# Halves of the first shift and scale, and one order of products at three attentions' openings, in a three-layer fp32 transformer kernel on one Trainium2 core

## What is computed

```
mod = silu(c) @ ada_w + ada_b;  shift, scale, gate = parts of mod
h = rms_norm(x, gain) * (1 + scale) + shift
x = x + gate * mixer(h)
```

```
logits = q @ k.T + bias (moba, swa), or + F[q] - F[k] (fox)
F = cumsum(log_sigmoid(h @ w_f + b_f))
attn = softmax(masked logits) @ v;  mixer = attn @ w_out
```

## Time and profile before

| what | value |
| --- | --- |
| median of three runs | 1499.24 us (1498.57 to 1499.58) |
| profiled execution, its own time | 1496.46 us |
| its span, first to last instruction | 1494.7 us |
| TensorE busy, mean granted clock | 1408.8 us, 0.982 |
| VectorE, ScalarE, POOL busy | 1085.8, 732.8, 140.3 us |
| moved by DMA | 333.63 MB, mean 223 GB/s |

### The profile page before, as it was taken

The page is one execution under the profiler, slowest core; times in us unless marked ns, Lnnn a source line. Parts: engine busy times, 40 slices in busy tenths (PEclk is TensorE's granted clock), DMA queues, the critical chain, the costliest instruction groups (busy, mean ns, idle before and its releaser), DMA issues.

```text
span 1494.7 us, 18521 instructions
## 1 busy us (share of the span) xinstructions
PE 1408.8 (94%) x7262; PEld 1165.3 (78%) x7262; DVE 1085.8 (73%) x1523; ACT 732.8 (49%) x1036; POOL 140.3 (9%) x199
## 2 busy tenths in 40 slices
PE   2799898999989999988999999999999899999998
PEld 1578888999968888765678887788887676788886
DVE  5857887998988998747478778788877446466444
ACT  3454446444564334667553445643337557554332
POOL 1100100111001221000011110011110100000000
PEclk9899999999999999998999999999999989999999
DMA  9775756877959998440378886688963631475552
GB/s 351 252 221 178 259 180 208 277 266 241 314 161 347 343 355 303 161 167 4 102 242 309 302 294 242 219 302 294 304 235 113 199 113 57 141 253 176 184 183 76
DMA packets 189289, 333.63 MB, mean 223 GB/s; under 512 B 8850, under 2 KB 132478, under 8 KB 188180
## 3 DMA queue, kind: packets, MB, share of 16 engines
q1 hardware_dynamic: 161392, 236.02, 46.9%
q0 software_dynamic: 27232, 96.21, 18.9%
q10 hardware_dynamic: 580, 0.23, 0.1%
HBM read 331.27 MB, written 1.15 MB: 222 GB/s over the span
## 4 chain that ended last, share of the span: by engine, by line
PE 77%; DVE 10%; ACT 5%; DMA 4%; issue 3%; SPq 0%; ACTq 0%; POOL 0%; DVEq 0%; POOLq 0%
PE bank L1473 10%; PE bank L1475 10%; PE bank L1474 10%; PE bank L1436 8%; PE bank L1438 7%; PE bank L1437 7%; DVE lo L968 4%; PE bank L1368 3%; PE bank L1369 3%; PE bank L1370 3%; DMA ada<-in_ada_w 2%; DVE ada_sum L926 2%; PE bank L1601 2%; PE bank L1603 2%; PE bank L1602 2%
## 5 line engine op out<-in xcount | busy, mean ns | idle before, releaser
L968 DVE TENSOR_TENSOR lo<-raw,hi 128x2048 fp32r<-128x2048 f32 x215 | 490.9, 2286 | 83.5 <-ACT hi L535 82.7
L535 ACT ACTIVATE hi<-raw 128x2048 fp32r<-128x2048 f32 x215 | 405.8, 1910 | 31.4 <-DMA raw<-in_w_out 21.1
L1473 PE MATMUL bank<-hi,h_hi 128*128 128x512 f32 x704 | 278.1, 395 | 3.6 <-DVE lo L968 1.9
L1475 PE MATMUL bank<-hi,h_lo 128*128 128x512 f32 x704 | 274.6, 390 | 0.0
L1474 PE MATMUL bank<-lo,h_hi 128*128 128x512 f32 x704 | 274.1, 389 | 0.0
L1436 PE MATMUL bank<-hi,o_hi 128*128 128x512 f32 x504 | 203.7, 404 | 11.6 <-DVE lo L968 9.5
L1438 PE MATMUL bank<-hi,o_lo 128*128 128x512 f32 x504 | 197.3, 391 | 0.0
L1437 PE MATMUL bank<-lo,o_hi 128*128 128x512 f32 x504 | 196.5, 390 | 0.0
L647 ACT ACTIVATE KT<-bank 128x256 f32<-128x256 f32 x88 | 33.8, 384 | 311.9 <-PE bank L1475 311.9
L1473 PEld LDWEIGHTS bank<-hi,h_hi 128*128 128x128 f32 x704 | 132.2, 188 | 33.3 <-DVE lo L968 3.8
L1475 PEld LDWEIGHTS bank<-hi,h_lo 128*128 128x128 f32 x704 | 132.1, 188 | 28.1
(11 more groups left out here) (213 smaller groups left out, 2012.6 us busy)
## 6 DMA issues: line engine op xcount, KB each, us to landing
raw<-in_ffn_w SPq DMA_DIRECT2D x176, 512.0 KB, 5.3
ada<-in_ada_w POOLq DMA_DIRECT2D x100, 512.0 KB, 5.7
raw<-in_ffn_w SPq DMA_DIRECT2D x44, 1024.0 KB, 6.5
V<-in_ada_w POOLq DMA_DIRECT2D x76, 512.0 KB, 5.6
raw<-in_w_up SPq DMA_DIRECT2D x22, 1024.0 KB, 5.8
raw<-in_w_in SPq DMA_DIRECT2D x16, 1024.0 KB, 6.9
raw<-in_fox_w_in SPq DMA_DIRECT2D x12, 1024.0 KB, 5.3
raw<-in_w_down SPq DMA_DIRECT2D x11, 1024.0 KB, 6.2
```

The lines of the kernel that those rows point to most:

```text
L535: nc.scalar.activation(hi[:, n % NS, :], raw[:, n % NS, :], ACT.Copy).then_inc(hi_ready, 1)
L968: nc.vector.tensor_tensor(lo[:, n % NS, :], raw[:, n % NS, :], hi[:, n % NS, :].bitcast(F32), ALU.subtract).then_inc(lo_ready, 1)
L1473: mm(bank[:, :], xk_hi, wh[:, i, :], start=k == 0, stop=False, skip_group_check=True)
L1475: ins = mm(bank[:, :], xk_lo, wh[:, i, :], start=False, stop=k == KD - 1, skip_group_check=True)
```

## The change

It has three parts.

1. *Opening.* The 8 MB of shift and scale are loaded and added in two halves by features: columns 0 to 511 of both for all 1024 rows (eight transfers of 512 KB in rows of 2 KB), then units 0 and 1, then columns 512 to 1023 into the same eight places, which lie no longer in the ring. Units 0 and 1 are now the first halves of the blocks for keys and for queries, units 2 and 3 their second halves. Tiles 0 to 3 of both blocks and both row halves are multiplied before the second half of scale and shift. Rows of constants are turned ahead of the input.
2. *The adaLN pieces of moba.* Eight of 24 leave `PIECES_AT` and stand after two norms, a unit and five of the heads' steps.
3. *Order in swa and fox.* Head transposes and evictions come earlier in the products, in the order that moba has; in swa four row tiles more are left to the first three head steps, the last two roots are taken in one instruction at step 3, and one set of `busy` products is gone; in fox the gate's product and its chain come first, and the step rows follow the logits in six steps of eight tiles.

The diff, cut to its core:

```diff
-ROWS_FROM = {"swa": 12, "fox": 16}
-ROWS_STEP = {"swa": 2, "fox": 7}
+ROWS_FROM = {"swa": 8, "fox": 16}
+ROWS_STEP = {"swa": (3, 3, 2), "fox": (8,) * 6}
...
-        for u0 in (2, 3, 4, 4, 5, 5, 6, 7, 8, 9, 10, 11, 12, 12, 13, 14, 14, 15, 16, 16, 17, 17, 18, 18):
+        for u0 in (2, 7, 8, 9, 10, 11, 12, 12, 13, 14, 15, 16, 16, 17, 18, 18):
...
-        SUMS_AT.update({w0 + u: 1 for u in (7, 9, 13, 17, 19, 22)})
-        COLS_AT.update({w0 + u: 1 for u in (8, 10, 14, 18, 20, 23)})
-        GATES_AT[w0 + 15], GATES_AT[w0 + 21] = (s0, 0), (s0, 1)
+        SUMS_AT.update({w0 + u: 1 for u in (7, 9, 11, 14, 18, 20)})
+        COLS_AT.update({w0 + u: 1 for u in (8, 10, 12, 15, 19, 21)})
+        GATES_AT[w0 + 16], GATES_AT[w0 + 22] = (s0, 0), (s0, 1)
...
-        pro = [raw[:, n, :] for n in range(1, 5)] + [
-            flat(V[:, :, :]), flat(QT[:, :, :]), flat(TB[:, 8:16, :]),
-            ada[:, :, :, :].rearrange("p a b c -> p (a b c)")]
+        pro = ([V[:, n, :] for n in range(2)] + [flat(QT[:, 4 * n:4 * n + 4, :]) for n in range(2)]
+               + [flat(TB[:, 8 + 4 * n:12 + 4 * n, :]) for n in range(2)] + [flat(ada[:, n, :, :]) for n in range(2)])
...
# SP
-                elif w:
-                    sp.wait_ge(pro_step, w)
...
-            for i in range(KD):
+            for i in range(2 * KD):
                 if i == 3:
                     sp.dma_start(x[:, :, :], a["x"][0].rearrange("(t p) d -> p t d", p=P)).then_inc(x_full, 16)
-                sp.dma_start(pro[i], a["ada_w"][0][P * i:P * (i + 1), 0:2 * D]).then_inc(pro_full[i], 16)
+                if i == KD:
+                    for m in range(2):
+                        load(m, *unit_source(0, m))
+                r, half = i % KD, i // KD
+                if half:
+                    sp.wait_ge(pro_step, r + 1)
...
# POOL, first pieces
-                        pool.wait_ge(pro_step, KD)
+                        pool.wait_ge(pro_step, 2 * KD)
...
# ScalarE, opening
+            act.wait_ge(rows_turned, 1)
+            nc.scalar.activation(cols[:, :], G[0][:, :], ACT.Copy).then_inc(cols_done, 1)
             for t in range(2):
                 normed(0, t)
...
             split_to(0)
-            modulated(0, 0)
-            modulated(0, 1)
+            opened(0)
+            opened(1)
             split_to(1)
+            opened(2)
+            split_to(2)
+            opened(3)
...
# ScalarE, swa steps
                         attention_step(s, t)
-                        if t == 0:
-                            block_root(s, 4)
-                        elif t == 2:
-                            block_evict(s, 4)
+                        if t == 2:
                             block_square(s, 5)
                         elif t == 3:
-                            block_root(s, 5)
-                        elif t == 5:
-                            block_evict(s, 5)
+                            block_roots(s, 4)
+                        elif t in (5, 6):
+                            block_evict(s, t - 1)
...
# VectorE, opening
             split_to(0)
-            split_h(0, 0)
-            split_h(0, 1)
+            split_opened(0)
+            split_opened(1)
             split_to(1)
+            for i in range(KD, 2 * KD):
+                pro_piece(i)
+            pro_columns(1)
+            split_opened(2)
+            split_to(2)
+            split_opened(3)
...
# VectorE, swa steps
-                            block_norm(s, 4 + t // 3)
+                        elif t == 4:
+                            block_norm(s, 4)
+                            block_norm(s, 5)
...
# TensorE, moba
-                    block_rows(s, 0, 0, 0, KD)
-                    block_rows(s, 0, 1, 0, KD)
+                    block_rows(s, 0, 0, 0, 4)
+
+                    pe.wait_ge(hf_ready, 1)
+                    turn_half(0, 1, 1, A[0])
+                    block_rows(s, 0, 1, 0, 4)
+                    block_rows(s, 1, 0, 0, 4)
+                    block_rows(s, 1, 1, 0, 4)
+                    pro_turn(1)
+                    block_rows(s, 0, 0, 4, KD)
+                    block_rows(s, 0, 1, 4, KD)
+                    block_rows(s, 1, 0, 4, KD)
                     turn_block(s, 0)
-                    block_rows(s, 1, 0, 0, KD)
+                    block_rows(s, 1, 1, 4, KD)
...
# TensorE, fox, behind the gate's product
+                    block_rows(s, 0, 1, 0, 4)
+                    turn_block(s, 0)
+                    block_rows(s, 0, 1, 4, KD)
                     block_rows(s, 1, 1, 0, 4)
-                    turn_block(s, 0)
+                    turn_block(s, 1)
...
# TensorE, head steps of swa and fox
                     if t == 0:
-                        step_rows(s, 0)
                         pe.wait_ge(bk_ready, N0[s] + 4)
                     attention_step(s, t)
                     if t in turns:
                         turn_block(s, 4 + turns.index(t))
-                    if t:
-                        step_rows(s, t)
-                    if kind == "swa" and 2 <= t < 9:
+                    step_rows(s, t)
+                    if kind == "swa" and 3 <= t < 9:
                         busy(3)
```

More of the change, by code:

```diff
@@ L292, in conv_bank, with unit_of_block, opening @@
             return G[half] if j else A[2 + half]
+        def unit_of_block(s, b, half):
+            return W0[s] + (2 * half + b if KINDS[s] == "moba" and b < 2 else 2 * b + half)
+        def opening(i):
+            return i % 2, i // 2
         def product_bank(s, b, t):
@@ L577, in modulated, with opened @@
                     ins.then_inc(hf_ready, 1)
+            def opened(i):
+                t, h = opening(i)
+                act.wait_ge(acol_ready, h + 1)
+                act.wait_ge(xt_done, 2 * t + h + 1)
+                if i >= 2:
+                    act.wait_ge(h_ready, i - 1)
+                src = A[0] if i == 3 else A[2 * t + h]
+                for n in range(4):
+                    k = 4 * h + n
+                    ins = nc.scalar.activation(hf[:, 4 * (i % 2) + n, :], src[:, P * n:P * (n + 1)], ACT.Identity,
+                                               bias=modc[:, 0, k:k + 1], scale=acol[:, 0, k:k + 1])
+                ins.then_inc(hf_ready, 1)
             def boundary(b):
@@ L675, in block_root, with block_roots @@
                                      scale=1.0 / HD).then_inc(bstd_ready, 1)
+            def block_roots(s, e):
+                act.wait_ge(bsum_done, N0[s] + e + 2)
+                nc.scalar.activation(hstd[:, :, :], hstd[:, :, :], ACT.Sqrt, bias=eps[:, 0:1],
+                                     scale=1.0 / HD).then_inc(bstd_ready, 2)
             def block_evict(s, e):
@@ L1259, in _ @@
                     block_norm(s, 0)
+                    pieces(1)
                     split_through(s, 4)
@@ L1271, in _ @@
                         attention_step(s, t)
+                        pieces(int(t in (1, 3, 5, 7, 9)))
                         if t in (0, 2, 4, 6, 8):
@@ L1418, in gate_rows, with turn_half @@
                 turned += 1
+            def turn_half(b, t, h, bank):
+                pe.wait_ge(xn_ready, 4 * b + 2 * t + h + 1)
+                for i in range(4):
+                    ins = nc.tensor.transpose(bank[:, P * i:P * (i + 1)], xn(t, h)[:, P * i:P * (i + 1)], ident[:, :])
+                ins.then_inc(xt_done, 1)
             def turn_x(b, t):
                 for h in range(2):
[L1422 to L1425 removed]
+                    turn_half(b, t, h, A[2 * t + h])
             def rows_times(w, tiles, xh, xl, t, k0, first, last, s):
@@ L1620, in step_rows @@
                 kind = KINDS[s]
-                first = ROWS_FROM[kind] + ROWS_STEP[kind] * t
-                for r in range(first, min(first + ROWS_STEP[kind], 2 * KD * (len(BLOCKS[kind]) - 2))):
+                first = ROWS_FROM[kind] + sum(ROWS_STEP[kind][:t])
+                for r in range(first, first + sum(ROWS_STEP[kind][t:t + 1])):
                     n = r // KD
@@ L1781, in _, with pro_turn @@
                    start=True, stop=True).then_inc(bias_sum, 1)
-            pe.wait_ge(c_done, 1)
-            for h in range(2):
+            turn_x(0, 0)
+            turn_half(0, 1, 0, A[2])
+            def pro_turn(h):
+                pe.wait_ge(pro_step, KD * (h + 1))
                 for part in range(2):
-                    if part == 0:
-                        pe.wait_ge(pro_step, KD)
                     if h:
@@ L1790, in _ @@
                     for i in range(4):
-                        first = D * part + 512 * h + P * i
+                        first = D * h + 512 * part + P * i
                         ins = nc.tensor.transpose((M, S)[part][:, P * i:P * (i + 1)], pro_sum[:, first:first + P], ident[:, :])
                     ins.then_inc(pro_turned, 1)
+            pro_turn(0)
             pe.wait_ge(bias_rows, 1)
```

131 lines of the change are left out of this document (69 added, 62 removed).

## The result

The changed kernel takes 1488.95 us (median of 4 runs, 1488.79 to 1490.36) against 1498.9 for the kernel before, a ratio of 0.9933 with an interval of 0.9918 to 0.9948. That is faster, by 10 us and not by the 30 that were forecast, and outside the range given. The profiled execution took 1490.36 us, span 1488.5.

What follows compares the result with a forecast made beforehand. TensorE, busy 94% of the span, was taken as the bound, with gain only in its idle time and lower clock. 10.4 + 4.5 + 6.5 + 9.0 = 30.4 us gave 1466.1 profiled, 1468.8 median; range about 1459 to 1478.

Steps and rivals of the forecast that it cites:

- D: Forgetting attention's opening: waits of 4.1 us and 6.8 of clock loss go, 1.5 stays uncovered; gain 9.0 us, ends 2 and 11.
- step 6: Forgetting attention's head step left without row tiles; logits waiting for the last head transpose's copy cost 1.5 us.
- rival (1): The lower clock moves to new gaps instead of going; total gain only 17 us, time 1482; chance 0.16.
- A: First stage's opening: first product at 29.7, first logits at 79.7 instead of 90.1; gain 10.4 us, bounds 6 and 13.
- B: First stage's tail: the 3.3 us wait for the pool branch's low part and its clock loss shrink; gain 4.5 us, ends 0 and 5.6.
- The twelve products: First stage's opening: the first twelve of TensorE's 48 first-half products, taken at 0.43 us each instead of 0.23.
- C: Sliding-window attention's opening: waits for maxima and copies and the clock loss shrink; gain 6.5 us, ends 3 and 10.
- The new wait at step 5: Window attention: TensorE waits 4.5 us for a copy, behind the joint root's table loads, root and high part on ScalarE.
- (2): In the opening the small constant rows land late, everything from the first scale on 7 us later; 1475.8; chance 0.12.
- (3): In the opening half transfers cost as much as whole ones, turning A into -4; 1483; chance 0.05.
- (4): adaLN pieces transfer one at a time, 7.2 us each, so the first stage waits; slower by 21.5 us, 1521; chance 0.03.
- more than 10 us of lower clock in the two later attentions: A named sign that the forecast is wrong, in the window and forgetting attentions.

Runs made afterwards that it cites:

- run 1: Changed kernel with the forgetting attention's row tiles 7 a step for six steps and 6 in the seventh, instead of 8 in six: 1471.2 us.
- run 2: Changed kernel, still 8 tiles a step, with VectorE's low part of unit 11 ahead of tile 6's norm at step 4 of the forgetting attention: 1481.8 us.
- run 3: Changed kernel with the whole forgetting attention as before the change, order and 7 tiles a step; the rest stays changed: 1478.4 us.
- run 5: Kernel before with only the adaLN pieces moved; shift and scale whole, both attentions as before: 1488.7 us.
- run 6: Kernel before with only the opening by halves; old pieces and old attentions: 1499.3 us.
- run 10: Run 1's kernel with the opening undone (shift and scale whole, old unit order, constant rows behind the input); pieces and attentions stay changed: 1472.4 us.
- run 4: Changed kernel with the first stage's adaLN pieces put back at their old places: 1504.2 us.
- run 11: Run 1's kernel with the window attention's high parts of weight unit 8 and the two after it a step later: 1472.1 us.
- run 9: Run 1's kernel with weight unit 2's high and low parts ahead of the second halves' work, its adaLN piece tied to unit 3: 1471.3 us.

## Why the prediction was wrong, point by point

**The step that failed is in D:** "step 6 has none, and its last head transpose is followed by logits that need its copy: 1.5 us uncovered". The place was right and the size was not. What stands on the path there is not the copy but head 7's maximum, behind a whole low part of 2.28 us, and behind the wait of 3.2 TensorE's clock is at its lower level for some 20 us: together 10.6 us by runs 1 and 2. The sum had 1.5 for the wait and nothing for the clock behind it, though rival (1) had named that danger. And the same list did harm at a place that I had not walked: two steps earlier it asks for unit 11 while VectorE stands 3.85 us in a norm. That is another 7 us. The price of the list was 18 us, not 1.5. With the list of before, D is +7.2 by runs 1 and 3 (6.5 between their marks, 7.8 against the kernel before), where 9.0 was forecast: the gaps and the clock stretch behind the forget rows did go.

**A and B** were forecast at 14.9 and are 9.3 in the profile of the change, 12.3 in run 1's. The size is off by 2.6 to 5.6 us, but the working was wrong in a way that the sum hides: I gave 10.4 to the halves and 4.5 to the pieces. Runs 5, 6 and 10 show the pieces worth 10.8 by themselves and the halves 0 to 1.2. I summed the chain from the first product on, as if TensorE's work ended it; the sentence that "the adaLN pieces on VectorE drop from seven to four in this stretch, which is what keeps it from being later" was the mechanism, and it got no price. By the first mark alone, the whole opening ends the stage at 254.6 with the old pieces and at 244.6 and 245.6 with the moved ones (runs 5 and 10). The opening by halves ends it at 257.9 and 263.1 with the old ones (runs 4 and 6) and at 242.4 to 245.4 with the moved ones.

Inside A the first product came at 32.74, not 29.7. The timelines of ScalarE, TensorE and VectorE in the changed kernel show the chain that I left out:

```profile
20.71 2.55 ACT L579 ACTIVATE work<-x,rms 128x512 f32<-128x512 f32 x4
...
20.95 2.72 PE L1841 MATMUL bank<-tn,rel 33*8 33x384 f32 x4 [0.78 <-ACT cols L792]
23.60 2.82 PE L1485 MATMUL bank<-ident,work 128*128 128x128 f32 x12
26.21 1.91 PE L1854 MATMUL bank<-ident,pro_sum 128*128 128x128 f32 x8
...
29.24 2.28 DVE L1004 TENSOR_TENSOR lo<-raw,hi 128x2048 fp32r<-128x2048 f32 x1
...
32.74 0.77 PE L1666 MATMUL bank<-hi,h_hi 128*128 128x512 f32 x1 [4.61 <-DVE h_lo L1051]
```

The halves' steps ended about 24, a little behind my 23.1. But the transposes of their sums stand on TensorE behind the input's transposes and these behind the bias products, so they began at 26.2, and unit 0's low part, queued on VectorE behind the scale, at 29.2. I had worked unit 0's parts from its landing alone. The second halves then were 3 us late with it (55.0 for 52.0): VectorE's eight steps for them ended at 46.8 and not at 43.7. The clock was no part of the miss. The twelve products that I had put at the lower clock ran at 1.00 (below), and in the stretch from 49.8 TensorE was idle for half of the time; its 4.99 busy us at 0.50 cost 2.5. I had 1.7 there and 2.4 for the twelve products. The third head transpose's wait was put at 2.1 and is 2.1. So the first logits came at 83.6 and not at 79.7: A brought 6.5 where 10.4 was forecast.

**B** brought 2.8 where 4.5 was forecast. The 3.3 us wait for the pool branch is gone, and 2.3 for a weight unit's low part came, behind three pieces' steps.

**C** held: 6.7 between the marks. The new wait at step 5 was forecast at 4.5 and is 3.4, for the reason given, ScalarE's table loads, root and high part; a second, 1.3, was not forecast.

**The rivals.** (1) The lower clock did move instead of going: the mean granted clock is 0.982 before and after; with the list put back, in run 1, it is 0.990. But the rival's prices are not borne out: C kept its gain, A and B brought 9.3 where it had 10, and D lost 9.5 instead of bringing 4, for two waits that the list of eight made. Its 1482 is nearer to 1489 than mine with only a part of the cause. (2) The constant rows: their transposes ran at 19.1, not at 31, so it falls. (3) Halves that cost as much as whole ones: unit 0's low part ended at 31.5 and the first product was 10 us earlier than before, so it falls; run 6's zero has another reason. (4) Slower, by one piece at a time: nothing of it is seen, and moving the pieces is what won.

On rival (3): what the Trainium skill (DMA: Bandwidth & Descriptors, Anatomy of one DMA) says of a fixed part of 2.0 us is measured on transfers that GpSimd issues; the halves are issued by SP. Paid in full by eight more transfers it would have made A about -5, and A is +6.5 at the first logits: the trace disagrees with that use of it.

Of the signs I had named, "more than 10 us of lower clock in the two later attentions" was the one that came.

## What to carry to other kernels

Take a list of how much work covers each step as seriously as an order: walk every step for what each engine has queued ahead of what the next step needs, also at the steps that seem to stay as they are. An edit that brings the first product forward is worth what it does to the engine that ends the stage; here that was VectorE, and moving eight small pieces out of its way did what the whole opening by halves did not. And undo each part by itself, since a kernel with several changes can hold an 18 us loss and still be faster.

## What the runs showed of the hardware

TensorE can stay at the lower of its two levels, 1.2 of 2.4 GHz, for a long time while it is busy: 17.10 us of 17.10 in run 11, shortly behind a wait of 1.3 us, and 21.30 of 21.30 at a mean of 0.52 in the changed kernel, behind one of 3.2. That wait cost some 10 us there, by runs 1 and 2.

Not every such wait has a stretch behind it. The first product stands behind a wait of 5.0 us in the kernel before and of 4.6 in the changed one. The clock behind it was 0.50 in the first profile and 1.00 in the second:

```profile
42.00:46.00 4.00, 3.32 (x8) 2.67 (x9) 3.10 (x6) 3.35 (x9) 1.02 (x2) 0.50 1.02 363
32.00:36.00 4.00, 3.26 (x8) 2.62 (x9) 3.52 (x4) 2.06 (x2) 0.00 (x0) 1.00 1.06 382
```

The stretches also differ from one execution to the next. The four executions of run 9 took 1468.9 to 1475.9 us, with a mean granted clock of 0.991 in the shortest and 0.986 in the longest; run 11 spread by 5.6 us in the same way. The kernel before spread from 1492.0 to 1505.9 over the groups. A fix of 2 us could not be told by four executions of each kernel; the wait itself could be read in each trace.
